# Hybrid decoder block on eight cores: block 3's and block 2's transposes on TensorE, weight loads ranked ahead of row copies in SyncE's queue, and a token-by-token end of block 0

## The reference

```
u = rms_norm(h, g_mix) @ w_in                       # 1024 -> 2576
c_val, c_gate, q, k, v, g, gate_lr = split(u)
y_conv = silu(LayerNorm(causal_depthwise_conv31(c_val * sigmoid(c_gate)) + b))      # 512 channels
y_gla  = per-head rms_norm(gated linear attention(q, k, v, gate_lr)) * silu(g)      # 4 heads, 512
h = h + concat(y_conv, y_gla) @ w_out               # output projection
x2 = rms_norm(h, g_ffn)                             # "next norm"
h = h + (silu(x2 @ w_ffn_gate) * (x2 @ w_ffn_up)) @ w_ffn_down                      # 1024 -> 2816 -> 1024
out = rms_norm(h, g_final)                          # meta positions dropped
```

## Time and profile before

| | |
|---|---|
| median of 3 runs | 1607.28 us (1602.62 to 1607.32) |
| the profiled execution | 1608.12 us, its slowest core's span 1606.6 us |
| spans of the 8 cores | 1574.1 to 1606.6 us |
| PE (matmul) busy | 1480.3 us, 92% of the span |
| DVE, ACT, POOL busy | 793.9, 520.2, 230.0 us |
| DMA transposes | 44, queue q10, 5.1% of 16 engines' span |
| chain that ended last | PE 76%, DMA 10%, SyncE's queue 5% |

### The profile page before, as it was taken

One profiled execution on the slowest core, in us unless ns is written; L12 is line 12 of the kernel. 1 busy time (PEld: TensorE's weight loads), 2 busy tenths in 40 slices (PEclk: granted clock), 3 DMA queues, 4 the chain that ended last, 5 costly groups with the idle time before them and its releaser, 6 DMA issues.

```text
span 1606.6 us, 26266 instructions; the slowest of 8 cores (1574.1 to 1606.6 us)
## 1 busy us (share of the span) xinstructions
PE 1480.3 (92%) x8098; PEld 678.4 (42%) x8098; DVE 793.9 (49%) x1685; ACT 520.2 (32%) x812; POOL 230.0 (14%) x294
## 2 busy tenths in 40 slices
PE   4885999989997699998999999999999989999994
PEld 1442444433443244443444434444444434444442
DVE  3547366423663246652475444743475443843423
ACT  3535342423322044222433144222432235211101
POOL 2042150102300014000320013000320003000000
PEclk8987999999999799999999999999999999999997
DMA  9987689998669885468634976368734975466641
GB/s 188 282 196 166 136 162 182 182 248 223 188 186 185 177 247 174 139 186 210 211 131 158 196 230 206 107 205 208 245 119 153 209 200 158 137 177 181 193 156 53
DMA packets 139832, 292.92 MB, mean 182 GB/s; under 512 B 59040, under 2 KB 75808, under 8 KB 139696
## 3 DMA queue, kind: packets, MB, share of 16 engines
q1 hardware_dynamic: 75664, 216.19, 44.6%
q0 software_dynamic: 17568, 63.51, 19.5%
q10 hardware_dynamic: 46464, 11.54, 5.1%
HBM read 254.16 MB, written 41.94 MB: 184 GB/s over the span
## 4 chain that ended last, share of the span: by engine, by line
PE 76%; DMA 10%; SPq 5%; issue 4%; DVE 2%; ACT 2%; POOL 0%; ACTq 0%; DVEq 0%; POOLq 0%
PE ps L642 57%; PE ps L1197 11%; SPq L768 4%; PE ps L819 3%; DMA xT<-xn_tm 3%; DMA wring<-wpack 3%; DMA wring<-wsc 2%; DMA out<-h 1%; ACT yT L610 1%; DMA wsc<-wring 1%; PE ps L724 1%; SPq L437 0%; PE ps L1086 0%; PE ps L1113 0%; PE ps L631 0%
## 5 line engine op out<-in xcount | busy, mean ns | idle before, releaser
L642 PE MATMUL ps<-x2T,wring 128*128 128x512 bf16 x2816 | 640.1, 381 | 16.3 <-DMA wring<-wsc 11.5
L642 PEld LDWEIGHTS ps<-x2T,wring 128*128 128x128 bf16 x2816 | 272.0, 98 | 353.8 <-issue 39.4
L1197 PE MATMUL ps<-wring,actT 128*128 128x512 bf16 x1408 | 313.0, 380 | 15.0 <-DMA wring<-wpack 8.9
L1181 DVE SCALAR_TENSOR_TENSOR ftmp<-ftmp,ps 128x512 f32<-128x512 f32 x176 | 119.9, 685 | 274.5 <-ACT ftmp L1180 274.4
L1180 ACT ACTIVATE ftmp<-ps 128x512 f32<-128x512 f32 x176 | 104.9, 596 | 351.7 <-PE ps L642 338.8
L1197 PEld LDWEIGHTS ps<-wring,actT 128*128 128x128 bf16 x1408 | 137.0, 98 | 185.6 <-issue 26.1
L642 PE MATMUL ps<-xT,wring 128*128 128x512 bf16 x736 | 169.2, 386 | 17.5 <-DMA xT<-xn_tm 17.5
L1183 DVE SCALAR_TENSOR_TENSOR actT<-ftmp,ps 128x512 bf16<-128x512 f32 x176 | 120.1, 686 | 40.9 <-PE ps L642 37.7
L642 PE MATMUL ps<-wring,xT 128*128 128x512 bf16 x512 | 129.2, 400 | 9.0 <-DMA wring<-wpack 7.6
L642 PEld LDWEIGHTS ps<-xT,wring 128*128 128x128 bf16 x736 | 72.4, 99 | 106.6 <-issue 25.2
L642 PE MATMUL ps<-wring,yT 128*128 128x512 bf16 x512 | 116.7, 379 | 0.0
(11 more groups left out here) (176 smaller groups left out, 1244.3 us busy)
## 6 DMA issues: line engine op xcount, KB each, us to landing
wring<-wsc SPq DMA_DIRECT2D x319, 512.0 KB, 4.9
wring<-wpack POOLq DMA_DIRECT2D x63, 512.0 KB, 9.5
wsc<-wring SPq DMA_DIRECT2D x46, 512.0 KB, 7.1
rep<-vT SPq DMA_DIRECT2D x256, 67.5 KB, 7.2
h<-xin POOLq DMA_DIRECT2D x28, 512.0 KB, 11.9
out<-h POOLq DMA_DIRECT2D x28, 512.0 KB, 7.1
h<-xin SPq DMA_DIRECT2D x4, 512.0 KB, 12.8
out<-h SPq DMA_DIRECT2D x4, 512.0 KB, 2.7
```

The lines of the kernel that those rows point to most:

```text
L642: ins = e.matmul(pt_ap, lhsT=lhs(kc), rhs=rhs(kc), start=(kc == 0), stop=(kc == KC - 1))
L1181: P.add("dve", lambda e: e.scalar_tensor_tensor(out=th[:], in0=th[:], scalar=1.0, in1=pg[:], op0=ALU.add, op1=ALU.mult), R=[Bpg, Bth], W=[ ...
L1197: ins = e.matmul(ps[t][:], lhsT=actT[:, j, t * 128:(t + 1) * 128], rhs=wd3[:, j - j0, :], start=(j == 0), stop=(j == NJ - 1))
```

## The change

Six edits:

1. `xT` of block 3 and `x2T` of block 2 are transposed on TensorE (`bi > 3` and `bi > 2`).
2. A load from `wsc` in SyncE's queue gets a rank 30 plan units lower than its place, so that where it and row copies or stores are ready together it goes first. The stores keep their ranks.
3. Block 0's order: `o0`, `o1` go between the convolution units, and the output projection goes token tile by token tile, each followed by that tile's own norm and transpose (`n0..3`), in place of `stats2` and the four `apply2`. The two halves of the output weights are held at once.
4. Block 1's first list is spread over 0.2 to 1.05 of block 0's second list, not 0.02 to 0.98.
5. In the schedule, the latency between two TensorE operations is 0, not 0.05.
6. `norm` of the meta tile gets slot NT (4, as before); block 0's new norms use slots 4 to 7.

```diff
-          "ktr sc0 kv sc1 conv0 conv1 conv2 conv3 ln o0 o1 y0 o2 y1 ln0 o3 y2 ln1 y3 ln2 ln3 "
-          "out00 out01 out02 out03 out10 out11 out12 out13"),
+          "ktr sc0 kv sc1 conv0 o0 conv1 o1 conv2 conv3 ln y0 o2 y1 ln0 o3 y2 ln1 y3 ln2 ln3 "
+          "out00 out10 n0 out01 out11 n1 out02 out12 n2 out03 out13 n3"),
...
-                lat = 0.05 if u.eng == e and not o.dma else (0.25 if e == "pe" else 0.12)
+                lat = 0.0 if u.eng == e == "pe" else 0.05 if u.eng == e and not o.dma else (0.25 if e == "pe" else 0.12)
...
-                    P.add("sp", lambda e: e.dma_start(out=dst, in_=wsc[tile]), R=[Bwsc[tile]], W=[B_], dkey=f"wh{sl}")
+                    op = P.add("sp", lambda e: e.dma_start(out=dst, in_=wsc[tile]), R=[Bwsc[tile]], W=[B_], dkey=f"wh{sl}")
+                    op.rank = (P.rank - 30.0, op.rank[1])
...
-                        transp(xni[t], xT[:, t], BxT[t], bi > 2)
+                        transp(xni[t], xT[:, t], BxT[t], bi > 3)
...
-                                wt_g["o"] = wget(W_O + 2 * cb, W_O + 2 * cb + 1)
-                            (w0, B0), (w1, B1) = wt_g["o"]
+                                wt_g["o", cb] = wget(W_O + 2 * cb, W_O + 2 * cb + 1)
+                            (w0, B0), (w1, B1) = wt_g["o", cb]
...
+                for t in range(NT):
+                    @unit(0.6, f"n{t}")
+                    def _(t=t):
+                        transp(norm(h[hs][t], Bh[hs][t], gffn, NT + t), x2T[:, t], Bx2T[t], False)
...
-                late.append((0.6, stats2))
-                for t in range(NT):
-                    def apply2(t=t):
-                        i = norm_apply(h[hs][t], Bh[hs][t], gffn, stt["n2"], 1, t)
-                        transp(i, x2T[:, t], Bx2T[t], bi > 1)
-                    late.append((0.6, apply2))
+                if bi:
+                    late.append((0.6, stats2))
+                    for t in range(NT):
+                        def apply2(t=t):
+                            i = norm_apply(h[hs][t], Bh[hs][t], gffn, stt["n2"], 1, t)
+                            transp(i, x2T[:, t], Bx2T[t], bi > 2)
+                        late.append((0.6, apply2))
...
-            side(mix[1][0], 0.02, 0.98)
+            side(mix[1][0], 0.2, 1.05)
```

More of the change, by code:

```diff
@@ L701, in _ @@
                         else:
-                            xni["m"] = norm(h[2][3], Bh[2][3], gmix, 4)
-                        transp(xni[t], xT[:, t], BxT[t], bi > 2)
+                            xni["m"] = norm(h[2][3], Bh[2][3], gmix, NT)
+                        transp(xni[t], xT[:, t], BxT[t], bi > 3)
                 pbank = early_ps if bi == 1 else mps
@@ L1142, in _ @@
                             if t == NT - 1:
-                                wdone(wt_g["o"])
+                                wdone(wt_g["o", cb])
+                for t in range(NT):
+                    @unit(0.6, f"n{t}")
+                    def _(t=t):
+                        transp(norm(h[hs][t], Bh[hs][t], gffn, NT + t), x2T[:, t], Bx2T[t], False)
                 def stats2():
```

## The result

The changed kernel takes 1584.45 us (median), against 1607.28: 22.8 us faster, ratio 0.985 [0.981, 0.989]. The forecast was 1571, with a range of 1556 to 1592. `L643` is now the matmul helper, `L632` the transposes on TensorE, `L1204` the weight-down matmuls, `L599` the product of a per-tile norm.

A forecast was written before the change was run, and what follows sets the result against it. TensorE was busy for 92% of the span, leaving its idle time and time at the lower clock to gain; terms 16 + 10 + 8 + 2 = 36 us off 1607.3 gave 1571 us, range 1556 to 1592.

The forecast's parts named there:

- (a): Block 1's feed-forward part: waits for weights replace those for transposes, passing loads give 2 us; total 1586 us, chance 0.17.
- (b): Block 0's mixer end wins nothing net; first gate/up matmul above 168 us would show it; total 1580 us, chance 0.13.
- main case: Whole kernel: 1571 us, own range 1558 to 1584, chance 0.56; its sign, first gate/up matmul near 156 to 160 us.
- block 0's end: Block 0's mixer end and projection: new order and per-tile norms gain 10 us, bounds 4 to 16.
- transposes: Block 1's feed-forward part: eight DMA transposes moved to TensorE gain 16 us, bounds 9 to 21.
- loads ahead of row copies: SyncE's queue at block boundaries: weight loads passing row copies gain 8 us, bounds 1 to 15.
- the end: Last weight-down tiles: with latency 0 only one addition is left at the end; gain 2 us, bounds 1.5 to 2.5.
- shortfall: Block 1's feed-forward part: without the waits, the stretch is 9.7 us too short for weight queues; half comes back.
- 131 in place of 140.15: Block 0's projection start: `o0`, `o1` among the convolutions let it start at 131 us, 9 us earlier.
- +1.4 for three transposes in the projection: Block 0's output projection: it now holds transposes of three finished tiles, costing 1.4 us.
- 7.1 in place of 18.53: Behind block 0's last projection matmul: one tile's norm, not four, takes 7.1 us, 11.4 us less.
- later `v` matmuls: Block 1's 24 `v` matmuls can't fill the gap after block 0's projection and come later, costing 5.2 us.

The follow-up runs named there:

- block0_undone: The changed kernel with block 0's order, norms and block 1's list spread (edits 3 and 4) put back as before; mean span 1564.2 us, ratio 0.980 and 0.982 to before.
- only_transposes: The kernel before with only block 3's `xT` and block 2's `x2T` transposed on TensorE (edit 1); ratio 0.985 to before, mean span 1575.5 us.
- only_latency: The kernel before with only the scheduled latency between two TensorE operations set to 0 (edit 5); ratio 1.000 to before, mean span 1594.0 us.
- only_block0: The kernel before with only block 0's new order, per-tile norms, norm slots and block 1's later spread (edits 3, 4, 6); ratio 1.004, mean span 1597.6 us.

## Why the prediction was right, and where not

The sign and the range held; the number is 13 us too low. The range held because it was drawn out to rivals (a) and (b): 1584.45 is just past the edge of the main case's own 1558 to 1584, and the main case's sign, a first gate/up matmul at 156 to 160, failed. At 177.2 it was rival (b)'s. One term makes the miss. For the other three I forecast 26 us, and `block0_undone`, which has them without block 0's end, is 27.8 faster; block 0's end was to give 10 and costs 6.5 there. By the terms of the sum:

| term | forecast | alone, on the mean span | what the stages show |
|---|---|---|---|
| transposes | -16 (-9 to -21) | -16.5 | block 1's part -21.5, blocks 2 to 6 +5.5 |
| block 0's end | -10 (-4 to -16) | +5.6 | first gate/up +1.9, block 0's part +3.9; outside its bounds |
| loads ahead of row copies | -8 (-1 to -15) | -6.7 | blocks 2 to 6 -7.4 |
| the end | -2 (-1.5 to -2.5) | +2.0 | tail -0.7 |
| sum | -36 | -15.6 (together -21.3) | |

**Transposes: right, with one step wrong and some luck.** I let half of a "shortfall" of 9.7 us come back as waits for weights. None came back: in block 1's whole part these waits fell from a mean of 9.8 us to 5.9 with edit 1 alone and 4.9 in the changed kernel, and the stage won 21.5, the whole of my upper bound. I had counted only the 5.3 us of such waits just ahead of the stall. The loss I had not seen is later, in blocks 2 to 6. That 16.5 came out where I said 16 is luck: a larger gain, less a loss that I hadn't in the sum. Whether that loss comes from the transposes still on the DMA isn't shown. TensorE's waits for them have a mean of 6.2 us in `only_transposes` and 2.1 before, but from 0.3 to 11.0 over its cores, and 4.6 in `only_latency`, which has before's transposes. The loss is gone where edit 2 is in too (884.9 in `block0_undone`), and the parts together give more than one by one: transposes, rank and latency alone sum to -21.2 +- 2.7, in one kernel they give -27.8 +- 0.7. What exactly links them I haven't shown. That earlier weight loads leave more of the DMA engines free when a transpose is issued is only argued. The engines' time that a transpose takes was the right thing to read: 37.3% for 1.31 MB. The Trainium skill (Advanced Engine Details and Errata, X-Bar Transpose) has transposing DMAs as fast as others; removing them took away the wait without giving it to the weights, which is what the factor of three in the trace foretold and the rule did not. The factor is that of this stretch, though. Over the whole span of the same core the page has:

```profile
q1 hardware_dynamic: 75664, 216.19, 44.6%
...
q10 hardware_dynamic: 46464, 11.54, 5.1%
```

That is 302 against 141 GB/s of the engines' time, a factor of two; from 722 to 762, without GpSimd's loads, q10 moves 0.52 MB in 9.4% of 40 us, 138 GB/s. So 85 GB/s is the figure of the crowded stretch, and not of a transpose as such.

**Block 0's end: the mechanism failed at three steps.** First, "131 in place of 140.15". I took the layer norm's chain to be held by `o0` and `o1` alone. It is still interleaved, on in-order engines, with the four `y` heads. Three rows of the changed kernel:

```profile
117.11 1.02 PE L865 MATMUL ps<-mtmp,ones 128*128 128x512 f32 x2
...
129.80 0.59 POOL L1164 DMA_DIRECT2D h<-xin  x1 [2.83 <-DVE sto L582]
...
141.06 0.69 DVE L963 SCALAR_TENSOR_TENSOR yT<-rep 128x512 bf16<-128x512 f32 x1 [1.54 <-ACT rep L962]
```

The layer norm's second sum runs at 117.11, after 16 `c0` matmuls which the planner put ahead of it (it ran at 113.07 before). GpSimd's queue holds an `h` load that waits 2.83 us for a VectorE step, with the last products behind it. The last layer-norm step is at 141.06, and the projection can only start then. Second, "+1.4 for three transposes in the projection". I priced them as work and not as waits. Each stands in TensorE's fixed order behind that tile's addition, square, seven small steps and product; of the 9.7 us that the projection lengthened by, 3.8 are such waits (2.56 + 1.26), 1.7 the transposes, and the rest, 4.3, matmuls at the lower clock: the granted clock is 0.75 over this stage, and the 8 matmuls at 157.20 take 0.45 us each where 56 in 12.25 take 0.22. Some 2 us of the 4.3 lie in the first 40 matmuls (10.87 us here, 8.79 on core 3 of `only_block0`), ahead of the first stop for a norm; the granted clock is 0.58 from 141.90 to 147.00, behind the short stops that end the mixer. Third, "7.1 in place of 18.53" behind the last matmul came out at 11.2. The last tile's addition stands behind the product of the tile before and starts at 167.95, 1.9 us after the last matmul; from it to the end of the product (173.23) it is 5.3; transposes, copy and the 8 `v` matmuls (3.21 us) take 4.0. The later `v` matmuls I costed at 5.2 are the one term that held in kind: 16 of the 24 come later, 3.5 us at 0.216. Rival (b) had this mechanism, but stopped at "wins nothing"; the bounds should have held a loss.

**Loads ahead of row copies: right.** Waits fell from 9.0 to 3.0 us on the mean core with this edit alone (on core 7 of the changed kernel it is 6.8, where I had said under 6; its mean core has 4.0). The queue shows the interleaving forecast.

**The end: too large.** I let "one addition 0.4 later" stand for the end of the chain. VectorE's order puts the last addition behind steps of the tile before, whose product of 1.28 us then goes ahead of the last tile's nine small steps.

**The slowest core.** I took the profiled core's waits off the median and let "none of the others comes out above this sum". In the changed kernel the cores differ in blocks 2 to 6 by TensorE's waits for the remaining DMA transposes of `xT` (0.3 to 10.2 us) and for weights (0.7 to 6.8), and the metric takes the worst of eight. The average core is at 1570.7; the metric is 13 above. Before, 15 above. That 1571 is also the average core's time is a coincidence; I forecast the slowest.

A kernel with edits 1, 2, 5 and 6 and block 0's end as before, or with the norms behind the projection, is the better one: 1577 us against 1584 on average, for either.

## What to carry to other kernels

Where each engine runs a fixed order, a step that is split per tile and interleaved with matmuls can cost the latency of its chain and not only its work, as here: leave one or two tiles of other matmuls between a tile's last matmul and the transposes that wait for its norm. A transfer kind that holds the DMA engines far longer than its bytes warrant should go first when the engines are full; once they aren't full, its remaining uses can cost less than TensorE's time to replace them, here by 8.6 us for 36 of them. With eight cores, compare kernels by the mean of the cores' spans as well: it told apart 6 us here that the slowest core's intervals left open.

## What was not expected of the hardware

Every core of one execution has its own waits for the same DMA transposes, 0.3 to 10.2 us in blocks 2 to 6, with the same instruction order and data shapes. With none left, those stages are within 2.6 us of each other on all eight cores.
